# Odd layer of a two-layer encoder: values as the stationary operand, split in two, and the row sums applied in the gate

## The reference

```python
def window_gqa_with_sink(q, k, v, sink, cos, sin):     # 32 query heads, 4 key/value heads of 64 features
    ...
    def one_block(args):                               # one block of 128 queries against its 3 neighbouring key blocks
        blk, qx, kx, vx = args
        s = jnp.einsum('bqhgd,bkhd->bhgqk', qx, kx) * scale
        s = jnp.where(valid, s, -jnp.inf)              # |i - j| <= 128
        m = jnp.maximum(jnp.max(s, axis=-1, keepdims=True), sink_g)
        p = jnp.exp(s - m)
        p = p / (jnp.sum(p, axis=-1, keepdims=True) + jnp.exp(sink_g - m))
        return jnp.einsum('bhgqk,bkhd->bqhgd', p, vx)
    ...

def odd_layer(x, norm_w, w_in, w_out, sink, cos, sin):
    h = rmsnorm(x, norm_w)
    qc, kc, vc, gc = split_cols(h @ w_in, ODD_SIZES)   # 2048, 256, 256, 2048 columns
    oc = window_gqa_with_sink(qc, kc, vc, sink, cos, sin) * jax.nn.silu(gc)
    return oc @ w_out
```

## Time and profile before

| | us |
|---|---|
| median of 3 runs | 1248.28 (1246.93 to 1252.05) |
| profiled execution, its own time | 1247.63 |
| its span, first to last instruction | 1245.8 |
| PE busy | 1174.2 (94%) |
| DVE busy | 921.0 (74%) |
| ACT busy | 589.2 (47%) |
| mean granted TensorE clock | 0.984 of 2.4 GHz |

### The profile page before, as it was taken

How to read it: one execution, slowest core, us unless ns; L and a number is a source line. 1 busy time by engine, 2 the same in 40 slices (tenths; PEclk the granted TensorE clock), 3 DMA queues, 4 the chain that set the end, 5 groups by cost and what they waited for, 6 DMA issues and landing times. The chain is left out here.

```text
span 1245.8 us, 18859 instructions
## 1 busy us (share of the span) xinstructions
PE 1174.2 (94%) x6028; PEld 952.0 (76%) x6028; DVE 921.0 (74%) x1777; ACT 589.2 (47%) x1086; POOL 0.2 (0%) x4
## 2 busy tenths in 40 slices
PE   5989999999999999999999967999999999999995
PEld 3767778778777787777787745888888888888884
DVE  6769778778778878787797768567667676756765
ACT  5364454553554544545544534345444344544442
POOL 0000000000000000000000000000000000000000
PEclk7999999999999999999999988999999999999999
DMA  6521512523314215215115003543221333212111
GB/s 190 152 68 51 136 52 65 138 67 72 113 51 122 63 51 135 67 51 135 51 51 142 28 1 90 119 130 91 51 84 51 101 79 89 84 51 84 51 35 67
DMA packets 131090, 102.98 MB, mean 83 GB/s; under 512 B 5360, under 2 KB 116336, under 8 KB 131056
## 3 DMA queue, kind: packets, MB, share of 16 engines
q1 hardware_dynamic: 131056, 102.54, 30.2%
HBM read 77.36 MB, written 2.10 MB: 64 GB/s over the span
## 5 line engine op out<-in xcount | busy, mean ns | idle before, releaser
L73 PE MATMUL bank_proj<-hH,w_hi 128*128 128x512 f32 x576 | 229.7, 399 | 3.8 <-DVE hL L139 3.8
L75 PE MATMUL bank_proj<-hH,w_lo 128*128 128x512 f32 x576 | 225.5, 392 | 0.0
L74 PE MATMUL bank_proj<-hL,w_hi 128*128 128x512 f32 x576 | 225.2, 391 | 0.0
L73 PEld LDWEIGHTS bank_proj<-hH,w_hi 128*128 128x128 f32 x576 | 108.8, 189 | 26.7 <-issue 5.3
L75 PEld LDWEIGHTS bank_proj<-hH,w_lo 128*128 128x128 f32 x576 | 108.6, 189 | 23.6
L74 PEld LDWEIGHTS bank_proj<-hL,w_hi 128*128 128x128 f32 x576 | 108.9, 189 | 21.5
L73 PE MATMUL bank_odd_proj<-hH,w_hi 128*128 128x512 f32 x288 | 119.5, 415 | 5.1 <-DVE hL L139 4.4
L75 PE MATMUL bank_odd_proj<-hH,w_lo 128*128 128x512 f32 x288 | 113.7, 395 | 0.0
L74 PE MATMUL bank_odd_proj<-hL,w_hi 128*128 128x512 f32 x288 | 112.9, 392 | 0.0
L968 DVE TENSOR_TENSOR w_lo<-w_raw,w_hi 128x1024 fp32r<-128x1024 f32 x73 | 88.9, 1219 | 20.0 <-ACT w_hi L565 20.0
L1473 ACT ACTIVATE probs<-bank_odd_score,small 128x256 f32<-128x256 f32 (+1 forms) x128 | 66.3, 523 | 78.3 <-DVE small L1607 77.5
(11 more groups left out here) (223 smaller groups left out, 2365.7 us busy)
## 6 DMA issues: line engine op xcount, KB each, us to landing
w_raw<-in_w_in_even SPq DMA_DIRECT2D x72, 512.0 KB, 4.5
w_raw<-in_w_in_odd SPq DMA_DIRECT2D x36, 512.0 KB, 4.7
qs<-parts SPq DMA_DIRECT2D x96, 128.0 KB, 2.3
ks<-parts SPq DMA_DIRECT2D x40, 256.0 KB, 4.3
o_raw<-in_w_out_even SPq DMA_DIRECT2D x16, 512.0 KB, 5.0
o_raw<-in_w_out_odd SPq DMA_DIRECT2D x14, 512.0 KB, 6.7
out<-w_raw SPq DMA_DIRECT2D x4, 512.0 KB, 2.6
mixT<-in_x SPq DMA_DIRECT2D x2, 512.0 KB, 5.6
```

The source lines that it names most:

```text
L73: pe.matmul(out, hi, moving_hi, start=start, stop=False)
L74: pe.matmul(out, hi, moving_lo, start=False, stop=False)
L75: return pe.matmul(out, lo, moving_hi, start=False, stop=stop)
```

## The change

The product of turned probabilities and values changes sides. The values become the stationary operand, with their high and low parts side by side (64 columns each), made once ahead of the loop. The turned probabilities of both heads move, 256 columns in one matmul, once their high and once their low part. Each result then has features on the partitions: rows 0 to 63 from the high values, rows 64 to 127 from the low values, for both heads. ACT makes the high part of both heads' turned probabilities, DVE the low part of both. ACT then copies two quarters of the result across the partition halves (`swap_halves`), DVE adds them to the other two (`add_halves`). The division by the row sums no longer happens on queries: ACT spreads the 8 columns of weights over 512 columns (`spread_weight`), PE turns that (`turn_weight`), DVE multiplies it with the gate (`apply_weight`) and that with the added result (`scale_y`). ACT takes over the high part of y (`high_y`), DVE keeps the low part (`low_y`).

```diff
-        v = sb("v2", [P, NC, 4 * HD])
+        v = sb("v2", [P, NC, 4, 2, HD], F32R)
-        probsT = sb("probsT", [P, 2, 2, 3 * P])
-        normed = sb("normed", [P, SEQ])
+        probsT = sb("probsT", [P, 2, 3, 2, P], F32R)
+        summed = sb("summed", [P, SEQ])
+        spread = sb("spread", [P, 2 * NC, HD])
...
# PE
-            def values(h, half, t):
+            def values(h, half, t, group):
                 lo, n = window(t)
-                if t == 0:
-                    if O.free.due(h, half):
-                        pe.wait_ge(O.free.sem, O.free.at(h, half))
+                if t % 2 == 0 and O.free.due(h, 2 * half + t // 2):
+                    pe.wait_ge(O.free.sem, O.free.at(h, 2 * half + t // 2))
                 for a in range(2):
                     pe.wait_ge(T[a].free.sem, T[a].free.at(h, tile_use(half, t)))
-                    col = (2 * t + a) * HD
-                    for j in range(n):
-                        mm = pe.matmul(O[:, col:col + HD], probsT[:, t % 2, a, j * P:(j + 1) * P],
-                                       v[:, lo + j, bass.ds(key_head(h, half) * HD, HD)],
-                                       start=j == 0, stop=j == n - 1)
-                if t == NC - 1:
+                at = O[:, (t % 2) * 2 * P:(t % 2 + 1) * 2 * P]
+                for j in range(n):
+                    value = v[:, lo + j, 2 * half + group].rearrange("p i f -> p (i f)")
+                    for part in range(2):
+                        mm = pe.matmul(at, value, probsT[:, part, j].rearrange("p a q -> p (a q)"),
+                                       start=j == 0 and part == 0, stop=j == n - 1 and part == 1)
+                if t % 2 == 1:
                     mm.then_inc(O.full.sem, 1)
-            def turn_out(h_before, before, use):
+            def turn_weight(h_before, before, use):
...
-                pe.wait_ge(O.free.sem, O.free.at(h_before, before + 1))
+                pe.wait_ge(spread_out.sem, spread_out.at(h_before, before + 1))
                 for t in range(NC):
-                    mm = pe.transpose(W[:, t * P:(t + 1) * P], normed[:, t * P:(t + 1) * P], eye[:])
+                    mm = pe.transpose(W[:, t * P:(t + 1) * P], spread[:, 2 * t:2 * t + 2].rearrange("p a f -> p (a f)"),
+                                      eye[:])
...
                 if not first:
-                    values(h_before, before, 3)
+                    values(h_before, before, 3, group if half else group_before)
+                    turn_weight(h_before, before, turn_of(half, outs))
                 if project:
                     proj(h, n, 1)
...
-                values(h, half, 0)
-                if not first:
-                    turn_out(h_before, before, turn_of(half, outs))
+                values(h, half, 0, group)
...
# ACT, in the order of its new half_step
                 if not first:
                     high_turn(h_before, before, 3)
                 if outs:
                     high_out(h - 1, 0)
                 soft_max(h, half, 0)
                 if not first:
                     spread_weight(h_before, before)
                 if outs:
                     high_out(h - 1, 1)
                 if not first:
                     swap_halves(h_before, before, 1)
                 if not last or not half:
                     high(h, n)
                 high_turn(h, half, 0)
                 if outs:
                     high_y(h - 1, 1)
                 soft_max(h, half, 1)
...
                 high_turn(h, half, 1)
                 soft_max(h, half, 2)
                 swap_halves(h, half, 0)
                 high_turn(h, half, 2)
                 soft_max(h, half, 3)
                 exp_sink(h, half)
...              # silu
                 if half:
                     high_y(h, 0)
# DVE, in the order of its new half_step
                 if not first:
                     low_turn(h_before, before, 3)
                 maxima(h, half, 0)
                 if not first:
                     weigh(h_before, before)
                 if not half and not first:
                     low_y(h - 1, 0)
                     low_out(h - 1, 0)
                     low_out(h - 1, 1)
                 if not first:
                     add_halves(h_before, before, 1)
                     apply_weight(h, before, use)
                     scale_y(h_before, before, h, use)
                 low_turn(h, half, 0)
                 maxima(h, half, 1)
                 if not half and not first:
                     low_y(h - 1, 1)
                 if not (last and half):
                     rotate(h, 2 * half + 1)
                 low_turn(h, half, 1)
                 maxima(h, half, 2)
                 if not zeroth:
                     add_out(h, range(4 * half, 4 * half + 1), 5 * half + 2)
                 add_halves(h, half, 0)
                 if lows:
                     low(h, 3 + 2 * half)
                 if not zeroth:
                     add_out(h, range(4 * half + 1, 4 * half + 2), 5 * half + 3)
                 low_turn(h, half, 2)
                 maxima(h, half, 3)
                 shift_sink(h, half)
...              # add_out, low, add_out as before
```

More of the change, by code:

```diff
@@ L1358, in _, with half_step @@
             pe.wait_ge(k_moved.sem, k_moved.at(0, 8))
-            def half_step(h, half, zeroth, last):
+            def half_step(h, half, group, group_before, zeroth, last):
                 n = 1 if half == 0 else 3
@@ L1388, in half_step @@
                     out_tile(h, 4 * half, 5 * half + 2)
-                values(h, half, 1)
+                values(h, half, 1, group)
                 if outs:
@@ L1521, in half_step @@
                 n = 3 + 2 * half
[L1522 to L1523 removed]
+                first, outs = zeroth and not half, not zeroth and not half
+                if not first:
+                    high_turn(h_before, before, 3)
+                if outs:
+                    high_out(h - 1, 0)
                 soft_max(h, half, 0)
[L1525 to L1526 removed]
+                if not first:
+                    spread_weight(h_before, before)
+                if outs:
                     high_out(h - 1, 1)
+                if not first:
+                    swap_halves(h_before, before, 1)
                 if not last or not half:
                     high(h, n)
[L1530 removed]
+                high_turn(h, half, 0)
+                if outs:
+                    high_y(h - 1, 1)
                 soft_max(h, half, 1)
```

140 lines of the change are left out of this document (81 added, 59 removed).

## The result

| | before | after |
|---|---|---|
| median, us | 1248.4 (1246.93 to 1252.05) | 1281.15 (1277.76 to 1286.09, 4 runs) |
| profiled execution, its own time | 1247.63 | 1286.09 |
| its span | 1245.8 | 1284.3 |
| mean granted TensorE clock | 0.984 | 0.971 |

A forecast was written before the change was run, and what follows sets the result against it. PE's list of work was taken to set the pace until another engine's queue is late. Terms 8.4 + 1.6 + 2.5 + 3.5 + 1.6 + 2.7 + 1.1 = +21 us on 1247.6 gave 1268.5, range 1251 to 1280.

The forecast's parts named there:

- wait B: Third output tile, each half: PE waits for DVE's add, delayed by swaps, adds and a weight tile's low part; 1.2 us.
- What PE saves: Values' products: one weight load per matmul at 0.125 us; PE saves 1.9 us a half, 25.3 with nothing late.
- slow-matmul rival: Rival: the new values' matmul takes 0.165 or 0.19 us; +12 us, 1280 in all; chance 0.04.
- split of the values ahead of the loop: Before the loop, one DVE instruction of 0.69 us each, under projections: costs 0, or 1.4 us uncovered.
- What the others get: Work added to ACT and DVE: DVE about 3.3 us more a half, busy about 20 and 24 us.
- Wait A: Turned weights in half 0: PE stands still for ACT's spread, behind table load and exponentials; 1.75 us.
- The rival of the held adds: Rival: each add pair loses two overlaps of 0.08 us, 16 times in the path, 2.7 us: 1271; chance 0.18.
- the rule quoted in the prediction: On DVE, an instruction whose input starts in another quadrant of partitions is held until every earlier one is done.
- Wait C: Fourth output tile, each half: PE waits for DVE's third add, behind low parts and maxima; 0.55 us.
- The ends of the loop: Zeroth step +2.5 and +3.5 us, step 1's wait at the turned weights 1.6 longer, last half +2.7, tail +1.1.
- The table load early: Rival: half 0's table load precedes its wait, the turned-weights wait shrinks by 1.28 to 0.5 us: -10, 1258.5; chance 0.14.

The follow-up runs named there:

- gate copied: Changed kernel with the gate copied instead of passed through SiLU, so ACT loads no function table in the loop: 1267.3 us, ratio 1.015.
- full partitions: Changed kernel with both swaps and both adds on all 128 partitions from partition 0, result not the reference's: 1271.5 us, ratio 1.018.
- Both: Changed kernel, weights spread ahead of maxima and exponentials, first weight tile's low part after the third output tile's add: 1258.2 us, ratio 1.007.
- all reorderings: Changed kernel, ACT's spread first, output weights' high parts after swaps; DVE's output-tile adds earlier, second low part in next half: 1256.0 us, ratio 1.005.
- table early: Changed kernel with the Exp table load issued right behind the fourth block's turned copies, in both halves: 1278.5 us, ratio 1.023.
- low weights later: Changed kernel with DVE's low part of the first weight tile moved behind the third output tile's add: 1263.3 us, ratio 1.012.

## Why the prediction was right in kind and short in size

The step that failed is a term of the sum, wait B: 1.2 us forecast, 1.7 measured, in each steady half. Its walk let an instruction begin 0.08 to 0.10 us before the end of the one ahead, and around the swaps and adds none does. The sum by its own terms, from the second execution of the changed kernel (loop and tail 475.1 against 444.6):

| term | forecast | measured |
|---|---|---|
| six halves 1 | -1.2 | +1.8 |
| halves 0 of steps 2 to 6 | +8.0 | +10.5 |
| half 0 of step 1 | +3.2 | +5.0 |
| zeroth step | +6.0 | +6.9 |
| half 0 of step 7 | +1.6 | +1.4 |
| last half | +2.7 | +3.3 |
| tail | +1.1 | +1.7 |
| sum | +21 (21.4 unrounded) | +30.5 |

- *What PE saves*: right. Groups of 4 take 0.60 (forecast 0.61); with the waits taken off (27.5 - 2.35, 29.3 - 1.75 - 2.35), a half is 25.2 us, forecast 25.3. The slow-matmul rival is out. The split of the values ahead of the loop shows no cost either, as forecast: the loop begins at 800.12, before at 801.25.
- *What the others get*: right. DVE is busy for 19.8 and 23.2 us (forecast 20 and 24), and instructions on 64 partitions last as long as on 128, 0.38 and 0.42.
- *Wait A*: right to 0.05 us in place and size, wrong if read as a price. Taken away by another order, it returned 0.6 of 1.75, since PE then stood behind the lists at the values and output tiles; made 1.45 shorter by a shorter list ("gate copied"), it returned 1.5. A wait's length is not what its removal gives.
- *Wait B*: the step that failed. "On DVE and ACT an instruction not waiting starts about 0.08 to 0.10 us before the end of the one ahead" does not hold around swaps and adds, and B is 1.7 instead of 1.2. This is 0.5 in each of the 11 steady halves of steps 1 to 6: the first two rows of the table are 5.5 us over their forecast, of 9.1 that were missing (30.5 against 21.4). The rival of the held adds had the mechanism and a third of its price: it counted two lost overlaps of 0.08 on DVE. The run on full partitions shows three on DVE, 0.12 each, and 0.28 on ACT, in all 0.62 on the way to that add, with the same number and width of instructions. By the rule quoted in the prediction (the Trainium skill, VectorE: DVE Perf Modes, section Two Vector instructions with no wait between them) the start partition is compared for PSUM and SBUF apart; so the third held instruction, the next reader of PSUM behind the low weights, was to be had from it. The trace agrees with the rule so read. On ACT the trace alone shows the loss.
- *Wait C*: 0.65 for 0.55. Half 1, forecast at 27.0 and so 0.2 shorter than before, is 27.5, 0.3 longer.
- *The ends of the loop*: zeroth, step 1, last half and tail cost 3.9 us more than forecast. Some of it may again be B or its like, which is not shown. It goes beside the granted clock, which the sum had taken as in before: 0.91 in half 0 of step 1, 0.92 in the last half, 0.87 in the tail, against 1.00, 1.00 and 0.92; 0.96 and 0.95 in the zeroth step against 1.00. The engine had stood in the stretch ahead of the first of these (busy 21.9 of 26.8 us in the zeroth half 1), and a mean between the levels says that it ran at 1.2 GHz for part of each. Where it did, in half 0 of step 1 of the second execution (857.1 to 860.4 at 0.50), matmuls of 512 columns start 0.43 us apart instead of 0.23:

```profile
857.15 0.63 PE L73 MATMUL bank_odd_proj<-hH,w_hi 128*128 128x512 f32 x1
857.58 0.63 PE L74 MATMUL bank_odd_proj<-hL,w_hi 128*128 128x512 f32 x1
```

  So a window's length times what its clock is short of 1.00 (0.09 x 32.5 = 2.9 in half 0 of step 1) is an estimate of the most that the clock can have cost: 2.2 us in the zeroth step, 2.9 in half 0 of step 1, 1.7 in the last half and 1.8 more than before in the tail, 8.6 of the 30.5. That is enough for all of the 3.9. "Both" and "all reorderings" show the same in the last half (0.79 and 0.86) while the steady halves stay at 1.00. How much of each end is clock and how much is chain stays open; no run held the clock while keeping the waits.
- *The table load early* was not what the kernel did; that a kernel without it gains near 10 is shown by the copied gate (-11); that moving it alone brings 0.6 in a half 0 and nothing to be told in the whole, by "table early".

So where did the time go? PE saved 1.9 us in 16 halves, 30 us, and the kernel lost 30 beside it, about 60 in all. The waits hold 7 x 1.75 (A) and 13 x 2.35 (B and C) in steps 1 to 7, 43 of these; the other 17 are the zeroth step, the ends and the lower clock, not parted here. Of B, one low part ahead of an add that PE needed is worth 15 us over the kernel ("low weights later"), the partition change 0.6 a half, about 9 from the loop on (465.6 against 475.1, "full partitions"). At the ends of the loop no reordering tried came near the kernel before: the best last half of a whole result was 21.1 against 17.8.

## What to carry to other kernels

When work moves from a bound engine to others that still have idle time, ask what stands in their lists between the new work and the next thing the bound engine needs: here one subtraction of 1.2 us at the wrong place cost 15 us, more than the changes of partition in all swaps and adds, 9. Do not read the length of a wait as its price, and test it by removing it: wait A gave back a third of its length or nearly all, by how it was removed. And walk the first and last passes of a loop by themselves: an exchange that wins in the steady step (53.25 against 54.4) can lose in the others: 4.2 us in the zeroth step, 6.3 in the last half, 2.7 in the tail.

## What the hardware showed unasked

- In the changed kernel against "full partitions", a change of the partitions on which instructions begin (0, then 64, then 0) takes away the usual overlap with the one ahead: about 0.12 us each time on DVE, for the next instruction that reads SBUF and again for the next that reads PSUM, and about 0.14 each on ACT.
- GpSimd takes 2.54 us (mean of 21) for a 128x1024 subtraction for which DVE takes 1.22, and DVE's product of two SBUF tiles lasts up to 2.3 instead of 0.69 us beside it; those with an input in PSUM stay at 0.69.
- The granted clock stayed at 1.00 in steady halves with 1 to 4 us of waits each (26.4 to 29.3 us long against 25.2 without), and was between 0.78 and 0.97 in half 0 of step 1, the last half and the tail. With the low weights on GpSimd it was 0.90 to 0.95 in three of the five halves 0 of steps 2 to 6, which took 31.8 to 32.9 us.
